# Scores with a contraction of 64 rows, issued in pairs on the two halves of the array

## What is computed

```python
s = jnp.einsum('bqhd,bmhd->bhqm', mq, mk) * (dh ** -0.5)          # memory, dh = 64
s = jnp.einsum('bnqhgd,bnkhd->bnhgqk', qb, kband) * (dh ** -0.5)  # sliding window, dh = 64
iscore = relu(jnp.einsum('bqhd,bsd->bqhs', qib, k_idx))           # index, 64 wide, 8 heads
iscore = jnp.einsum('bqh,bqhs->bqs', wb, iscore)
_, sel = lax.top_k(iscore, topk)
```

## Time and profile before

| | |
|---|---|
| median of three runs | 2207.93 us |
| profiled execution | 2203.41 us |
| its span, first to last instruction | 2201.9 us |
| TensorE busy | 2077.1 us, 94% of the span |
| VectorE busy | 1161.8 us, 53% |
| ScalarE busy | 867.1 us, 39% |
| mean granted TensorE clock | 0.977 of full speed |

### The profile page before, as it was taken

One profiled execution on the slowest core, in us unless ns is written; L12 is line 12 of the kernel. 1 busy time (PEld: TensorE's weight loads), 2 busy tenths in 40 slices (PEclk: granted clock), 3 DMA queues, 4 the chain that ended last, 5 costly groups with the idle time before them and its releaser, 6 DMA issues.

```text
span 2201.9 us, 24613 instructions
## 1 busy us (share of the span) xinstructions
PE 2077.1 (94%) x9984; PEld 1692.5 (77%) x9984; DVE 1161.8 (53%) x2252; ACT 867.1 (39%) x1553; POOL 242.8 (11%) x185
## 2 busy tenths in 40 slices
PE   6999999999988999999999999999999799999797
PEld 6987888887876777788887878878778566877575
DVE  5427543332245666453333237998874438766553
ACT  5437432222232466442222222477552223365520
POOL 1002100000020000010000002776700000000000
PEclk9999999999999999999999999999999899999898
DMA  6321132223322121222322322222313221211211
GB/s 233 115 96 38 50 106 96 96 96 105 115 83 108 59 78 68 96 89 97 101 100 84 114 94 99 96 77 77 106 63 110 76 70 65 77 39 39 77 58 57
DMA packets 28800, 192.60 MB, mean 87 GB/s; under 512 B 3264, under 2 KB 3408, under 8 KB 7440
## 3 DMA queue, kind: packets, MB, share of 16 engines
q1 hardware_dynamic: 24848, 175.96, 23.4%
q0 software_dynamic: 3264, 12.99, 1.7%
q10 hardware_dynamic: 576, 2.10, 0.2%
HBM read 186.84 MB, written 4.19 MB: 87 GB/s over the span
## 4 chain that ended last, share of the span: by engine, by line
PE 80%; DVE 12%; ACT 5%; issue 1%; DMA 1%; POOL 0%; SPq 0%; DVEq 0%; ACTq 0%; POOLq 0%
PE bank L398 23%; PE bank L400 22%; PE bank L399 22%; DVE bank L2124 4%; PE bank L1810 2%; DVE WL L370 1%; ACT WH L356 1%; PE bank L1798 1%; PE bank L1701 1%; PE bank L1711 1%; PE bank L2265 1%; PE bank L1276 1%; PE bank L543 1%; PE bank L1187 1%; PE bank L1803 1%
## 5 line engine op out<-in xcount | busy, mean ns | idle before, releaser
L398 PE MATMUL bank<-XH,WH 128*128 128x512 f32 (+1 forms) x1504 | 596.0, 396 | 15.7 <-DVE XL L559 10.3
L400 PE MATMUL bank<-XH,WL 128*128 128x512 f32 (+1 forms) x1504 | 566.4, 377 | 0.0
L399 PE MATMUL bank<-XL,WH 128*128 128x512 f32 (+1 forms) x1504 | 566.1, 376 | 0.0
L370 DVE TENSOR_TENSOR WL<-RAW,WH 128x2048 fp32r<-128x2048 f32 x128 | 293.2, 2291 | 452.1 <-ACT WH L356 452.1
L356 ACT ACTIVATE WH<-RAW 128x2048 fp32r<-128x2048 f32 x148 | 282.2, 1908 | 328.1 <-PE bank L400 322.4
L398 PEld LDWEIGHTS bank<-XH,WH 128*128 128x128 f32 x1504 | 285.4, 190 | 85.5 <-issue 25.6
L399 PEld LDWEIGHTS bank<-XL,WH 128*128 128x128 f32 x1504 | 285.8, 190 | 55.5 <-issue 6.6
L400 PEld LDWEIGHTS bank<-XH,WL 128*128 128x128 f32 x1504 | 285.1, 190 | 52.9 <-issue 0.8
L2124 DVE SCALAR_TENSOR_TENSOR bank<-conv_in,cols,bank 128x512 f32<-128x512 f32 x290 | 198.2, 749 | 1.1
L398 PE MATMUL bank<-WH,XH 128*128 128x512 f32 (+2 forms) x416 | 157.5, 379 | 8.1 <-DVE XL L559 6.3
L399 PE MATMUL bank<-WL,XH 128*128 128x512 f32 (+2 forms) x416 | 153.2, 368 | 0.0
(11 more groups left out here) (333 smaller groups left out, 2974.4 us busy)
## 6 DMA issues: line engine op xcount, KB each, us to landing
RAW<-weights SPq DMA_DIRECT2D x164, 1024.0 KB, 4.8
row_a<-rows POOLq DMA_DIRECT2D x7, 512.0 KB, 6.0
row_b<-rows POOLq DMA_DIRECT2D x6, 512.0 KB, 6.3
x_res<-x SPq DMA_DIRECT2D x1, 2048.0 KB, 16.9
kv<-mem_park POOLq DMA_DIRECT2D x2, 1024.0 KB, 5.2
out<-x_res ACTq DMA_DIRECT2D x4, 512.0 KB, 2.6
mem_tok<-mem SPq DMA_DIRECT2D x1, 1024.0 KB, 5.0
mem_tok<-mem POOLq DMA_DIRECT2D x1, 1024.0 KB, 8.4
```

The source lines that it names most:

```text
L370: dve.tensor_tensor(WL[j][:, :], RAW[j][:, :], WH[j][:, :].bitcast(F32), ALU.subtract).then_inc(*lo.mark())
L398: pe.matmul(ps, ah, bh, start=first, stop=False)
L399: pe.matmul(ps, ah, bl, start=False, stop=False)
L400: return pe.matmul(ps, al, bh, start=False, stop=last)
```

## The change

- Index: at an even head the scores of heads k and k+1 are issued one behind the other, at an odd head none.
- Layer 2 of the first block: at an even step the scores of jobs i and i+1 are issued one behind the other (`SLIDE_PE` drops the odd ones); the score part moves into `slide_scores_pe`, unchanged.
- First mixer: an even memory head takes the next one with it. For this the third mLSTM job and the first memory job of each tile change places, so that heads 0 and 1 of the memory are neighbours in `FIRST_JOBS`. This order holds for all engines; beyond it only TensorE's order changes.

```diff
     FIRST_JOBS = [(kind, 4 * t + h) for t in range(NT) for kind, h in
-                  (("lstm", 0), ("lstm", 1), ("mem", 0), ("lstm", 2), ("mem", 1), ("lstm", 3), ("mem", 2), ("mem", 3))]
+                  (("lstm", 0), ("lstm", 1), ("lstm", 2), ("mem", 0), ("mem", 1), ("lstm", 3), ("mem", 2), ("mem", 3))]
...
                 if kind == "mem":
-                    if stage != 1:
-                        memory_job_pe(stage, i, j, 0, lambda c: mqT[:, c, :], ring)
+                    if stage == 0 and j % 2 == 0:
+                        memory_job_pe(0, i, j, 0, first_query, ring)
+                        memory_job_pe(0, i + 1, j + 1, 0, first_query, ring)
+                    elif stage > 1:
+                        memory_job_pe(stage, i, j, 0, None, ring)
                     continue
...
+    SLIDE_PE = [[(stage, i) for stage, i in step if stage or i % 2 == 0] for step in SLIDE_ORDER]
...
-        for n, step in enumerate(SLIDE_ORDER):
+        for n, step in enumerate(SLIDE_PE):
...
                 if stage == 0:
+                    slide_scores_pe(i)
+                    slide_scores_pe(i + 1)
...
     def index_step_pe(k, t):
-        if k < IH:
-            w, r = (t + 1) * P, slice(IHD * (k % 2), IHD * (k % 2) + IHD)
-            ps = take_bank("spare", "index", t, k)
-            pe.matmul(ps[:, 0:w], qiT[r, k // 2, t * P:(t + 1) * P], kiT[r, 0:w], start=True, stop=True).then_inc(
-                *T.mark("full", "index", t, k))
+        if k < IH and k % 2 == 0:
+            w = (t + 1) * P
+            for k in (k, k + 1):
+                r = slice(IHD * (k % 2), IHD * (k % 2) + IHD)
+                ps = take_bank("spare", "index", t, k)
+                pe.matmul(ps[:, 0:w], qiT[r, k // 2, t * P:(t + 1) * P], kiT[r, 0:w], start=True, stop=True).then_inc(
+                    *T.mark("full", "index", t, k))
```

More of the change, by code:

```diff
@@ L1136, in beside_first_pe, with first_query @@
             out_block_pe(t, b, q)
+    def first_query(c):
+        return mqT[:, c, :]
     def mlstm_pe():
@@ L1689, in sliding_pe @@
                 stage, i = step[k]
[L1690 to L1694, removed]
-                if stage == 0:
[L1696 to L1702, removed]
+                if stage == 0:
+                    slide_scores_pe(i)
+                    slide_scores_pe(i + 1)
+                elif i < 16:
+                    memory_job_pe(stage, i, i, 1, None, "six")
@@ L1703, in sliding_pe @@
                 elif stage == 2:
                     PE.wait_ge(*after("swa_recip", i - 16))
-                    turn_scores_pe(("swa", i - 16), S_of(i, SEQ, 1), w, "six")
+                    turn_scores_pe(("swa", i - 16), S_of(i, SEQ, 1), band(SWA[i - 16][0]), "six")
                 elif stage == 3:
+                    t, h = SWA[i - 16]
                     PE.wait_ge(*after("emptied", "turn", "swa", i - 16))
                     ps = take_bank("six", "swa_out", i - 16)
-                    n_keys = w // P
+                    n_keys = band(t) // P
@@ L1710, in sliding_pe, with slide_scores_pe @@
                     for c in range(n_keys):
                         mm = pe.matmul(ps[:, 0:HD], T_of(i, SEQ, 1)[:, c * P:(c + 1) * P],
-                                       kv_tok[:, t - n_keys + 1 + c, 256 + g * HD:256 + (g + 1) * HD],
+                                       kv_tok[:, t - n_keys + 1 + c, 256 + h // 3 * HD:256 + (h // 3 + 1) * HD],
                                        start=c == 0, stop=c == n_keys - 1)
                     mm.then_inc(*T.mark("full", "swa_out", i - 16))
+    def slide_scores_pe(i):
+        if i < 16:
+            memory_job_pe(0, i, i, 1, lambda c: qT[:, 6 + c, :], "six")
+            return
+        t, h = SWA[i - 16]
+        g, w = h // 3, band(t)
+        r = slice(64 * (h % 2), 64 * (h % 2) + 64)
+        keys = kT if h % 2 == g % 2 else kT_swapped
+        if (t, h) == (0, 2 * LATE_BLOCKS[0]):
+            PE.wait_ge(*after("emptied", "qT", LATE_BLOCKS[-1]))
+        ps = take_bank("six", "swa", i - 16)
+        pe.matmul(ps[:, 0:w], qT[r, h // 2, t * P:(t + 1) * P], keys[r, g // 2, (t + 1) * P - w:(t + 1) * P],
+                  start=True, stop=True).then_inc(*T.mark("full", "swa", i - 16))
```

## The result

The changed kernel takes 2170.12 us (median of four runs, 2169.18 to 2171.84), the kernel before 2207.18 us in the same comparison. The ratio is 0.9833, with a 95% interval of 0.9818 to 0.9848: 37.1 us less. I forecast 2179.2 with a range of 2172 to 2195, so the kernel is faster than the range allows. The profiled execution fell from 2203.41 to 2169.18 us (34.2 less), its span from 2201.9 to 2167.7.

What follows compares the result with a forecast made beforehand. TensorE's own queue was taken as the bound. Terms 20.8 + 11.2 + 1.2 - 3.0 - 1.5 = 28.7 us took the profiled 2203.4 to 2174.7; with 4.5 more for the median, 2179.2 us, range 2172 to 2195.

Steps and rivals of the forecast that it cites:

- (a): All 52 pairs: each enters and leaves the 64-row mode once instead of twice; 20.8 us saved, bounds 0 and 20.8.
- (b): All pairs: second score's first matmul (b1) runs beside first score's second (a2); 11.2 us saved, bounds 0 and 22.4.
- full overlap: Rival: both partners of a pair side by side from the first pass; 39.9 us saved, 2168.0 us; chance 0.07.
- (c): Starts of layer 2 and index: pairs at half clock save more; 1.2 us, bounds 0 and 3.
- (e): Layer 2: VectorE's long steps show where two or three meet; 1.5 us lost, bounds 0 and 4.
- (d): First mixer: TensorE waits for a bank that ScalarE's exponential still reads; 3.0 us lost, bounds 0 and 4.9.
- (f): Index: earlier scores feed ScalarE and VectorE earlier, selection still ends ahead of TensorE; 0 us lost.
- slower: Rival: in both mixers second scores wait for their banks, delaying everything behind; 6.8 us slower, 2214.7; chance 0.06.

Runs made afterwards that it cites:

- e8: The changed kernel, but in the index both partners of a pair use rows 0 to 63; 2181.40 us, ratio 0.9898 to the kernel before.
- e2: The kernel before with only layer 2's scores issued in pairs; 2180.09 us, ratio 0.9876.
- e7: The changed kernel, but the first mixer's paired scores have two banks of their own, other results a ring of four; 2158.57 us, ratio 0.9794 to the kernel before.
- e6: The changed kernel, but ScalarE does the first mixer's memory exponentials ahead of its copies in each step; 2160.61 us, ratio 0.9801 to the kernel before.
- e5: The kernel before with only the first mixer's job order changed, no scores paired; 2207.36 us, ratio 1.0016.
- e1: The kernel before with only the index's scores issued in pairs; 2191.25 us, ratio 0.9928.
- e3: The kernel before with only the first mixer changed, job order and pairs; 2213.58 us, ratio 1.0021.

## Why the prediction was wrong

**(a) Switching: right.** Forecast 0.40 us a pair and free passage between the halves. A pair of scores on the same rows takes 1.06 us with one entry and one exit (e8), and the index stage there is 5.4 us shorter, where (a) gave 4.8 and the pair at half clock a few tenths more. The forecast took this term at its upper bound for want of a row, and it came out there.

**(b) Overlap: the step that failed.** I took the middle, three passes for four, 11.2 us; the runs show two for four, the upper bound of 22.4, and more. My picture was that a1 a2 b1 b2 start in that order, so that only a2 and b1 meet. After shows otherwise: the piece is as long as one score. The timeline of the weight loads at a pair with 384 columns (start, duration, idle time before it) has all four loads done in 0.30 us, while one pass takes 0.325, so the partner's weights don't wait for a pass of the first score:

```profile
1784.44 0.30 PEld L2284 LDWEIGHTS bank<-kiT,qiT 64*128 64x128 f32 x4 [0.35 <-issue]
```

Nor do its matmuls wait for the first score's second one. A pair of layer 2 whose partners read different keys shows it by the names. In the queue both matmuls with `kT_swapped` stand ahead of both with `kT`, but they start in turn:

```profile
821.52 0.48 PE L1729 MATMUL bank<-kT_swapped,qT 64*128 64x256 f32 x1
821.52 0.48 PE L1729 MATMUL bank<-kT,qT 64*128 64x256 f32 x1
821.84 0.38 PE L1729 MATMUL bank<-kT_swapped,qT 64*128 64x256 f32 x1
821.84 0.38 PE L1729 MATMUL bank<-kT,qT 64*128 64x256 f32 x1
```

b1 starts beside a1, 0.32 us ahead of a2, and b2 beside a2: "a2 stands ahead of b1 in one queue", the argument against full overlap, doesn't hold for matmuls on different halves.

From e8 to after the index gains 8.9 us for the different rows; 1.6 of it is the clock, (c), and 7.3 is left, where the half share was 3.9 and the full one 7.8. Also, the six pairs with 128 columns, which I put at 0 since loads would leave nothing, take 0.42 us, what one would (0.20 + 0.22): another 1.3 us. The whole term is then 22.4 + 1.3 = 23.7, 12.5 more than forecast. The rival "full overlap" was given 0.07. Its price, 2168.0 us, is 2.1 from the median; its size of the overlap is the one that the runs show, but the rest of its sum, (c) to (e), was off in both directions, so that the small distance is partly luck. I weighed it by the order in the queue, for which I had no row; between bounds 0 and 22.4 with no row near either, the honest thing would have been to give both ends a like chance. By the Trainium skill (TensorEngine Tiling (Array Packing), Key Properties and Theoretical Speedup) tiles load and multiply in parallel, and with a dimension of at most 64 the speedup is up to two. The traces agree, with 0.63 us for two scores on different halves in after and 1.06 for two on the same rows in e8.

**(c) Half clock: right in kind, too small.** The first pair of the index takes 1.16 us at half clock, what one score took at the start of layer 2. But the larger part is one that I had only in the bound of 3 us: the stretch at half clock ends sooner. Three rows of the index's start (before, e8, after) and one of layer 2's start (after, against 0.53 from 749 to 759 before), with the clock behind the five busy times:

```profile
1778.00:1784.00 6.00, 6.00 (x15) 4.21 (x14) 0.35 (x1) 0.38 (x1) 0.00 (x0) 0.52 0.30 124
1759.00:1765.00 6.00, 6.00 (x14) 3.91 (x13) 0.84 (x2) 0.77 (x2) 0.00 (x0) 0.50 0.38 154
1761.00:1767.00 6.00, 6.00 (x29) 4.46 (x28) 0.34 (x1) 0.76 (x3) 0.00 (x0) 1.00 0.00 0
757.00:763.00 6.00, 5.13 (x38) 4.00 (x37) 3.38 (x15) 1.78 (x7) 0.00 (x0) 1.00 0.02 8
```

The index stage is at half clock for its first 5.8 us before and 5.7 in e8, and for 2.5 in after. Layer 2 is so for its first 10.2 us before and 3.4 in after, and not at all in e2 and e7. Half of each difference is time gained: 1.6 and 3.4 us, together 5.0 for the 1.2 of the forecast, over the bound. It goes with the pairs in every run: in the seven profiled executions with pairs on different halves in the index the stage is at half clock for 2.4 to 3.5 us, in the six others for 5.7 to 6.0; in the eight with pairs in layer 2 for 0 to 6.2 us at its start, in the five others for 9.6 to 10.2. Why the clock comes back sooner isn't shown.

**(d) The first mixer's banks: right mechanism and place, too small.** I named the first output product of a tile's second half, for the bank that the exponential reads, with 0.8, 0.8 and 1.4 us. The trace (duration of the piece, in brackets the idle time before it):

```profile
186.09 0.92 PE L1178 MATMUL bank<-proj,Tl 128*128 128x192 f32 x4 [0.93 <-ACT Sl L1300]
...
204.91 1.24 PE L1178 MATMUL bank<-proj,row_b 128*128 128x192 f32 x6 [0.81 <-ACT Sl L1300]
...
228.50 1.57 PE L1178 MATMUL bank<-proj,Tl 128*128 128x192 f32 x8 [1.50 <-ACT Sl L1300]
```

0.93, 0.81 and 1.50: 3.2 us for 3.0. What I left out are the other takes of banks read only a step before. I had counted 55 of them and priced the worst one in each tile. Six more waits cost 4.2 us. And a wait costs more than its length: TensorE's work in this stage should have fallen by 8 x (0.40 + 0.43) = 6.6 us, but the stage grew by 3.8, so 10.4 were lost for the 3.0 of the forecast. The idle time is up by 6.6 of that (8.1 for 1.5 in 80 us), and the 3.4 us at half clock cost 1.7. The other 2 us or so fit the products behind the waits, which are longer than their like. The output product behind the first wait above takes 0.92 us for four records, another one with nothing to wait for takes less:

```profile
189.47 0.67 PE bank L1178 x4
```

That is 0.25 us more, and there are ten waits (the nine and one of 0.6 on VectorE). This part is worked out from one pair of lines and not shown by an experiment of its own. What speaks for it: TensorE's busy time in the stage, the time at half clock counted half, falls by 4.5 us in after, and by 5.5 in e6 and 6.2 in e7, where the waits on the exponential are gone, against the 6.6 that the pairs save. The bound of 4.9 on (d) was wrong too: waits may cost more than the edit brings, since the new order alone already cost 2.9 in the profiled execution of e5.

**(e) Layer 2: too small.** Forecast 1.5 lost. Work saved is 12.8 for switching and 5.6 x 2 + 1.3 = 12.5 for overlap, 25.3 together. The stage shrank by 24.1, which looks like a loss of 1.2, but 3.4 of the 24.1 came from the clock, (c). Without it 20.7 are left, and 4.6 were lost, over the bound of 4. e2 and e7 bear it out: 116.9 us with no time at half clock, and after's 118.4 less 1.7 for its 3.4 us at half clock is 116.7. Of the 4.6, 1.8 are idle time of TensorE (4.6 us for 2.8, with waits of 0.9 and 0.9 on VectorE's reciprocals and 0.8 on ScalarE); the other 2.8 no run takes apart. Two steps should take 3.8 us; two of them take 3.60 (817.99 to 821.59).

**(f) The index behind it: right.** 14.9 us in the runs of e1, 14.4 in its stage; the selection gives nothing back.

**Sum.** Against the forecast (b) gives 12.5 more, (c) 3.8 more, (d) 7.4 less and (e) 3.1 less, together 5.8; the profiled executions differ from the forecast by 5.5 (34.2 for 28.7). The median differs by another 3.6, since that of after lies 0.9 above its profiled execution and not 4.5. So one step failed by its mechanism, (b), which had three passes where the runs show two; (c), (d) and (e) had the right kind and the wrong size. That (c) and (e) nearly cancel is luck. The rival "slower" had the second score wait for its own bank. That didn't come: in the first mixer none of the idle times of 0.2 us or more before TensorE's matmuls stands before a score of the memory. What came is its mirror, others waiting for the bank that the second score took, at 1.3 us a pair in the first mixer (10.4 over 8), over the 0.83 from which the rival decides; in layer 2 the loss is 0.14 a pair.

## What to carry to other kernels

Two products with half of the rows each (here float32, of 128 to 512 columns), on different halves and next to each other in the queue, cost what one does: look for such neighbours first, and count both the switching and the whole second product. Whatever is issued earlier also holds its bank from earlier on; go through the ring for every taker, not the worst, and give the early results banks of their own, or put their reader first in its engine's queue (here 7 to 8 us in a stage of 78; both together gave no more). Price an order and the edit that needs it apart: here the order alone cost 2.9 us of the 6.6 that the pairs of that stage save. And read the granted clock before you book a difference of stage lengths to work or to waits.

## What the runs showed of the hardware that was not expected

**Two float32 products of 64 rows overlap wholly**, passes and loads, at 128, 256, 384 and 512 columns (0.42, 0.63, 0.85, 1.06 us for two). Their matmuls don't start in the order of the queue: the second product's first one starts with the first product's first one (821.52 us), 0.32 us ahead of the first product's second.

**With the pairs the clock comes back sooner.** The index stage begins with 2.4 to 3.5 us at the 1.2 GHz level where its pairs lie on different halves, and with 5.7 to 6.0 where there are none or they share their rows (e8); layer 2 with 0 to 6.2 us for 9.6 to 10.2. It was worth 5.0 us of the 34.2.

**A short wait can cost the clock, and doesn't always.** In e3 layer 2 has the same wait as before the change (0.8 us on `DVE WL L391`). In e3 the clock fell to the 1.2 GHz level behind it and stayed there until 836 us, though TensorE was busy without a gap:

```profile
821.62 0.70 PE L1710 MATMUL bank<-kT,qT 64*128 64x256 f32 x2 [0.78 <-DVE WL L391]
```

```profile
820.00:822.00 2.00, 1.22 (x8) 0.72 (x6) 1.82 (x9) 2.00 (x7) 0.00 (x0) 1.00 0.00 0
822.00:824.00 2.00, 2.00 (x12) 1.66 (x10) 1.10 (x7) 1.01 (x5) 0.00 (x0) 0.73 0.72 168
...
834.00:836.00 2.00, 2.00 (x10) 2.00 (x11) 1.11 (x5) 1.69 (x5) 0.00 (x0) 0.50 0.02 8
836.00:838.00 2.00, 2.00 (x12) 1.51 (x11) 0.51 (x3) 0.00 (x1) 0.00 (x0) 0.86 0.00 0
```

It cost 5.9 us in that execution (148.4 for 142.5); layer 2 took 148.4 in e5 too, and in no other profiled execution did it get longer. In what a drop at one wait differs from no drop at another like it stays open. It makes the medians of e3 and e5, whose runs reach from 2202 to 2215 and 2224, less sharp than their stages.
